# The first stage of a fused two-block transformer kernel, reordered: where the condition row, the squares, the weight splits and the first transfers are done

## The reference, cut to what matters

```python
c_act = silu(c)                                    # c: one row of 1024
mod = (c_act @ w_ada + b_ada).reshape(1, 3, 3, 1024)   # shift, scale, gate of 3 sublayers
u = rmsnorm(h, norm1_g) * (1 + mod[:, 0, 1]) + mod[:, 0, 0]
g, up = split(u @ w_gu_1, 2)                       # 1024 -> 2 x 2816
h = h + 0.5 * mod[:, 0, 2] * ((silu(g) * up) @ w_down_1)
u = modulate(rmsnorm(h, norm2_g), mod[:, 1, 0], mod[:, 1, 1])
proj = u @ w_mix_in                                # queries, keys, values, convolution, gates
```

## Time and profile before

| | |
|---|---|
| time, median of 3 runs | 2076.58 us |
| profiled execution: its time / span | 2077.91 us / 2075.9 us |
| TensorE busy | 2039.7 us (98%) |
| VectorE / ScalarE / GpSimd busy | 53% / 39% / 6% |
| chain that ended last | TensorE 91%, VectorE 3%, issue 2%, DMA 1% |
| mean granted clock | 0.993 |

### The profile page before, as it was taken

The page is one execution under the profiler, slowest core; times in us unless marked ns, Lnnn a source line. Parts: engine busy times, 40 slices in busy tenths (PEclk is TensorE's granted clock), DMA queues, the critical chain, the costliest instruction groups (busy, mean ns, idle before and its releaser), DMA issues.

```text
span 2075.9 us, 25090 instructions
## 1 busy us (share of the span) xinstructions
PE 2039.7 (98%) x10215; PEld 1706.4 (82%) x10215; DVE 1101.8 (53%) x1681; ACT 804.4 (39%) x1252; POOL 116.0 (6%) x139
## 2 busy tenths in 40 slices
PE   6999999999999999999999999999999999999997
PEld 4788888888878898888889887778888988888887
DVE  8744444577753553333335646665425475456546
ACT  4422232355554343222323436555323353234334
POOL 3100000200000010000002000000000100000012
PEclk8999999999999999999999999999999999999999
DMA  7744534443433223233222332222333232332241
GB/s 278 254 165 158 177 137 134 152 142 121 142 94 101 92 75 108 76 112 106 89 70 90 119 122 72 73 81 92 102 99 94 72 102 83 111 102 95 71 149 41
DMA packets 71202, 236.27 MB, mean 114 GB/s; under 512 B 8864, under 2 KB 11168, under 8 KB 70704
## 3 DMA queue, kind: packets, MB, share of 16 engines
q1 hardware_dynamic: 68912, 226.59, 32.6%
q0 software_dynamic: 2032, 7.90, 1.3%
q10 hardware_dynamic: 144, 0.18, 0.0%
HBM read 229.89 MB, written 4.75 MB: 113 GB/s over the span
## 4 chain that ended last, share of the span: by engine, by line
PE 91%; DVE 3%; issue 2%; DMA 1%; ACT 1%; POOL 1%; DVEq 0%; SPq 0%; POOLq 0%; ACTq 0%
PE bank L678 81%; PE bank L742 4%; PE bank L1086 1%; PE bank L1072 1%; PE bank L968 1%; PE bank L859 1%; PE bank L862 1%; DVE raw_m L1635 1%; POOL ssq L2257 0%; DMA w_raw<-in_w_gu_dram 0%; PE bank L998 0%; DMA w_raw<-in_w_mix_dram 0%; PE bank L773 0%; DVE w_raw L1635 0%; PE bank L1118 0%
## 5 line engine op out<-in xcount | busy, mean ns | idle before, releaser
L1639 DVE TENSOR_TENSOR w_lo<-w_raw,w_hi 128x1024 fp32r<-128x1024 f32 (+2 forms) x367 | 418.2, 1167 | 202.1 <-ACT w_hi L1183 201.5
L678 PE MATMUL bank<-u_hi,w_hi 128*128 128x512 f32 (+1 forms) x1920 | 497.6, 372 | 7.1 <-ACT ple_s L1361 3.5
L678 PE MATMUL bank<-u_lo,w_hi 128*128 128x512 f32 (+1 forms) x1920 | 495.5, 371 | 7.0 <-DVE u_lo L1939 4.9
L678 PE MATMUL bank<-u_hi,w_lo 128*128 128x512 f32 (+1 forms) x1920 | 495.8, 370 | 0.0
L1183 ACT ACTIVATE w_hi<-w_raw 128x1024 fp32r<-128x1024 f32 (+2 forms) x368 | 347.2, 976 | 257.6 <-PE bank L678 193.4
L678 PEld LDWEIGHTS bank<-u_hi,w_hi 128*128 128x128 f32 x1920 | 358.0, 190 | 68.9 <-ACT ple_s L1361 3.9
L678 PEld LDWEIGHTS bank<-u_lo,w_hi 128*128 128x128 f32 x1920 | 357.5, 189 | 68.6 <-DVE u_lo L1939 5.7
L678 PEld LDWEIGHTS bank<-u_hi,w_lo 128*128 128x128 f32 x1920 | 357.3, 189 | 58.4
L1767 DVE TENSOR_TENSOR ff_a<-ff_s,bank 128x512 f32<-128x512 f32 x44 | 30.2, 687 | 224.0 <-issue 211.7
L1259 ACT ACTIVATE act_hi<-ff_a 128x512 fp32r<-128x512 f32 x66 | 41.7, 632 | 257.9 <-DVE ff_a L1767 217.8
L678 PE MATMUL bank<-act_lo,w_hi 128*128 128x512 f32 (+1 forms) x561 | 131.1, 379 | 0.0
(11 more groups left out here) (275 smaller groups left out, 2083.5 us busy)
## 6 DMA issues: line engine op xcount, KB each, us to landing
w_raw<-in_w_gu_dram SPq DMA_DIRECT2D x127, 512.0 KB, 3.9
w_raw<-in_w_ada_dram SPq DMA_DIRECT2D x66, 512.0 KB, 4.5
w_raw<-in_w_dn_dram SPq DMA_DIRECT2D x48, 384.0 KB, 3.1
w_raw<-in_w_mix_dram SPq DMA_DIRECT2D x36, 512.0 KB, 3.6
w_raw<-in_w_dn_dram SPq DMA_DIRECT2D x48, 320.0 KB, 3.2
w_raw<-in_w_in_dram SPq DMA_DIRECT2D x24, 512.0 KB, 3.7
w_raw<-in_w_o_dram SPq DMA_DIRECT2D x16, 512.0 KB, 3.5
w_raw<-in_w_in_g_dram SPq DMA_DIRECT2D x16, 512.0 KB, 3.6
```

What stands on the lines that cost most here:

```text
L678: m = e.matmul(bank[b][:, c], w, (x.lo if part == 2 else x.hi)[:, k, c], start=start, stop=stop, skip_group_check=True)
L1639: e.tensor_tensor(lo_of(name), raw_of(i), f32(hi_of(name)), ALU.subtract).then_inc(*s_w_lo.inc(name))
```

## The change

The condition row is loaded as one row by ScalarE's queue, put through silu there, and spread over the partitions by TensorE (two matmuls with a row of ones) and two VectorE copies. ScalarE squares all chunks into buffers of their own, VectorE adds them in four pairs, TensorE sums the pairs over partitions (16 small matmuls). VectorE's `first_normed` multiplies by the inverse norm alone; ScalarE computes the gain, applies scale and shift in one pass, and rounds; VectorE subtracts for all d. GpSimd does none of these any more. The first ring has 13 buffers and is used twice; the gate and up part of the first sublayer then uses a ring of eight, all later ones the ring of four. The embed weights and 1g3, 1u3 get split buffers of their own. TensorE gets matmuls on the identity (`warm`) at four places, and the order of the first groups is written out. In the stream 1g3 and 1u3 come ahead of the three "a" items; four "a" items now stand behind mv0 to mv3.

The diff, cut:

```diff
-N_MORE = 14
+N_MORE = 9
+FIRST_STREAM = (("pt", "ple0", "a", "a", "ple1", "1g0", "1u0", "a", "a", "1g1", "1u1", "a", "a", "1g2", "1u2")
+                + 10 * ("a",) + ("1g3", "1u3"))
+FIRST_STEPS = ((0, 0), ("embed", 7), ("warm", 8), (0, 1), (1, 0), (1, 1), ("warm", 6), (2, 0), (2, 1),
+               *[(g, k) for k in range(2, 8) for g in range(3)])
...
                     weight(f"{tag}u{m}", io[w_gu][NFF + m])
-                between()
+                    between()
...
-    ffn_tiles("1", "w_gu_1", "w_dn_1", first=3, between=some_ada)
+    ffn_tiles("1", "w_gu_1", "w_dn_1", first=4, between=some_ada)
     for j in (12, 16, 13, 17):
         weight(f"m{j}", io["w_mix"][j])
     for k in range(4):
         weight(f"mv{k}", io["w_mix_v"][k])
+        some_ada()
```

TensorE (`open_bank(b)` waits for whoever frees the bank; a bank written by `embed(d)` is free once ScalarE's `embed(d)` has copied it out):

```diff
+        def warm(n, b):
+            open_bank(b)
+            q.wait_ge(s_ident, 0)
+            for _ in range(n):
+                e.matmul(bank[b][:, 0:P], ident[:, :], ident[:, :], start=True, stop=True, skip_group_check=True)
+
         def embed(d):
-            b = banks.next()
+            b = banks.next() if d < 7 else 7
...
-            frees[b] = [(s_embed_dve if d < 2 else s_embed_act, d)]
+            frees[b] = [(s_embed, d)]
...
+        warm(16, 5)
+        q.wait_ge(s_crow, 0)
+        for x in range(2):
+            m = e.matmul(bank[6 + x][:, :], one_row[:, :], c_row[:, T * x:T * (x + 1)], start=True, stop=True,
                          skip_group_check=True)
...
+        warm(12, 5)
+        embed(0)
+        embed(1)
+        for k in range(0, ND, 2):
+            q.wait_ge(s_ssq_dve, ("n0", k))
+            for i in range(NB):
+                m = e.matmul(bank[7][:, i:i + 1], first_sq[:, k, P * i:P * (i + 1)], ones[:, :], start=k == 0 and i == 0,
...
+        embed(2)
...
+        for d in (3, 4, 5, 6):
             embed(d)
...
+        for g, i in FIRST_STEPS:
+            if g == "warm":
+                warm(i, 7)
+            elif g == "embed":
+                embed(i)
+            else:
+                if g == len(groups):
+                    groups.append(first_group(g))
+                groups[g](i)
```

ScalarE:

```diff
+        def first_high(d):
...
+            e.activation(gmul[:, d:d + 1], mod[:, g:g + 1], ACT.Identity, scale=vec("norm1_g", d),
...
+            q.wait_ge(s_u0, ("n0", d))
+            q.wait_ge(s_ada, c)
+            e.activation(x, x, ACT.Identity, scale=gmul[:, d:d + 1], bias=mod[:, c:c + 1]).then_inc(*s_u_hi.inc(("n0+", d)))
+            q.wait_ge(s_u_hi, ("n0+", d))
+            e.activation(u_hi[:, d, :], x, ACT.Copy).then_inc(*s_u_hi.inc(("n0", d)))
+
+        split_hi()
+        embed(0)
+        split_hi()
+        first_high(0)
+        embed(1)
         embed(2)
         embed(3)
         split_hi()
         split_hi()
+        first_high(1)
+        embed(4)
+        embed(5)
+        split_hi()
+        split_hi()
+        embed(6)
+        first_high(2)
+        first_high(3)
+        embed(7)
+        first_high(4)
+        first_high(5)
+        split_hi()
+        first_high(6)
+        split_hi()
+        first_high(7)
```

VectorE:

```diff
+        prepare_up_to("ple0")
+        for x in range(2):
+            q.wait_ge(s_out, ("c", None))
+            e.tensor_copy(cact[:, T * x:T * (x + 1)], bank[6 + x][:, :]).then_inc(*s_cact.inc(x))
+        for d in range(0, ND, 2):
...
+            e.tensor_tensor(a, a, b, ALU.add).then_inc(*s_ssq_dve.inc(("n0", d)))
...
+        prepare_up_to(mod_col(0, 1, 0))
         q.wait_ge(s_rt, ("n0", 0))
         e.reciprocal(inv[:, :], rt[:, :]).then_inc(*s_inv.inc(("n0", 0)))
+        prepare_up_to("ple1")
+        first_normed(0)
+        prepare_up_to(mod_col(0, 0, 1))
+        first_low(0)
+        prepare_up_to(mod_col(0, 1, 1))
+        first_normed(1)
+        prepare_up_to("1u1")
+        first_low(1)
+        prepare_up_to(mod_col(0, 1, 2))
+        first_normed(2)
+        prepare_up_to(mod_col(0, 0, 3))
+        first_low(2)
+        prepare_up_to(mod_col(0, 1, 3))
+        for d in range(3, ND):
+            first_normed(d)
+            prepare_up_to(mod_col(0, 1, d + 1) if d < ND - 1 else "1u3")
+            first_low(d)
```

More of the change, by code:

```diff
@@ L25 @@
 N_RAW = 4
-N_MORE = 14
+N_MORE = 9
 N_SPLIT = 6
-N_DVE = 3
+N_EARLY = 3
 VEC = {}
@@ L518, in block_kernel, with raw_place @@
     size = {x[1]: x[3] for x in stream}
-    by_pool = ("1g0", "1u0", "1g1", "1u1", "1g2", "1u2")
-    def raw_of(i):
-        n = stream[i][3]
-        return raw_more[i][:, 0:n] if i < N_MORE else w_raw[(i - N_MORE) % N_RAW][:, 0:n]
+    raws = raw_more + w_raw + raw_ffn
+    wide = (9, 10, 11, 12, 8, 13, 14, 15)
+    first_end = 2 * (N_MORE + N_RAW)
+    wide_end = first_end + (stream_index["1u21"] + 1 - first_end) // len(wide) * len(wide)
+    def raw_place(i):
+        if i < first_end:
+            return i % (N_MORE + N_RAW)
+        if i < wide_end:
+            return wide[(i - first_end) % len(wide)]
+        return N_MORE + (i - wide_end) % N_RAW
+    def raw_of(i):
+        return raws[raw_place(i)][:, 0:stream[i][3]]
+    raw_before, split_place, split_before = {}, {}, {}
+    last_at = {}
+    for i in range(len(stream)):
+        raw_before[i] = last_at.get(raw_place(i))
+        last_at[raw_place(i)] = i
+    last_at = {}
+    ring = [name for name in names if name not in EARLY]
+    for name in names:
+        split_place[name] = N_SPLIT + EARLY[name] if name in EARLY else ring.index(name) % N_SPLIT
+        split_before[name] = last_at.get(split_place[name])
+        last_at[split_place[name]] = name
+    hi_tiles, lo_tiles = w_hi + x_hi, w_lo + x_lo
     def hi_of(name):
-        return w_hi[split_index[name] % N_SPLIT][:, 0:size[name]]
+        return hi_tiles[split_place[name]][:, 0:size[name]]
     def lo_of(name):
-        return w_lo[split_index[name] % N_SPLIT][:, 0:size[name]]
+        return lo_tiles[split_place[name]][:, 0:size[name]]
     def split_end(name):
-        return min(split_index[name] + 1 + N_SPLIT, len(names))
+        j = split_index[name] + 1
+        while j < len(names) and (split_before[names[j]] is None or split_index[split_before[names[j]]] <= split_index[name]):
+            j += 1
+        return j
     def stream_end(name):
@@ L909, in first_group @@
             return outer(["1" + x for x in FIRST_OUTS[2 * g:2 * g + 2]], first_u, banks, glu_freed("1"))
[L911 to L917 removed]
+        groups = []
+        for g, i in FIRST_STEPS:
[3 more added lines that the diff above has]
+                embed(i)
+            else:
+                if g == len(groups):
+                    groups.append(first_group(g))
+                groups[g](i)
         def constant(x):
@@ L1897, in vector_program @@
         e.memset(eps[:, :], EPS).then_inc(*s_const.inc("eps"))
+        e.memset(one_row[:, :], 1.0).then_inc(*s_const.inc("row"))
         for i, x in enumerate((1.0, EPS, 1.0)):
             e.memset(sum_w[:, i:i + 1], x).then_inc(*s_const.inc(("sum_w", i)))
-        prepare()
-        prepare()
-        for d in range(ND):
-            add_square("n0", d)
-            if d in (4, 6):
-                i = d // 2 - 2
-                q.wait_ge(s_out, (("emb", i), None))
-                e.tensor_copy(ple_s[0][:, i, :], psum(("emb", i))[:, :]).then_inc(*s_embed_dve.inc(i))
@@ L1908, in vector_program, with first_normed, first_low @@
-        prepare()
-        q.wait_ge(s_cact, 0)
+        def first_normed(d):
+            q.wait_ge(s_out, ("inv", "n0", 0))
+            if d >= 4:
+                q.wait_ge(s_u_lo, ("n0", d - 4))
+            e.tensor_tensor(u0_full[d % 4][:, :], hres[:, d, :], bank[6][:, :], ALU.mult).then_inc(*s_u0.inc(("n0", d)))
+        def first_low(d):
+            q.wait_ge(s_u_hi, ("n0", d))
+            e.tensor_tensor(u_lo[:, d, :], u0_full[d % 4][:, :], f32(u_hi[:, d, :]),
+                            ALU.subtract).then_inc(*s_u_lo.inc(("n0", d)))
@@ new lines, in prepare_up_to @@
+        def prepare_up_to(name):
+            while done["stream"] <= stream_index[name]:
+                prepare()
+        prepare_up_to("ple0")
[3 more added lines that the diff above has]
+        for d in range(0, ND, 2):
+            a, b = first_sq[:, d, :], first_sq[:, d + 1, :]
+            q.wait_ge(s_sq, ("n0", d + 1))
+            e.tensor_tensor(a, a, b, ALU.add).then_inc(*s_ssq_dve.inc(("n0", d)))
@@ L2413, in sync_program @@
             e.dma_start(hres[:, 2 * i:2 * i + 2, :], io["xt"][:, 2 * i:2 * i + 2, :]).then_inc(*s_x[i].inc(0, by=16))
-        e.dma_start(cact[:, :], io["c"].to_broadcast([P, D])).then_inc(*s_c.inc(0, by=16))
-        load_beyond("1u3")
+        while done["load"] <= stream_index["1u6"]:
+            load()
         for i in range(2):
-            q.wait_ge(s_ple_out, i)
+            q.wait_ge(s_ple_out[i], 0)
         e.dma_start(ws_s[:, :, :], io["ws"]).then_inc(*s_ws_in.inc(0, by=16))
```

186 lines of the change are left out of this document (67 added, 119 removed).

## The result

| | before | after |
|---|---|---|
| median, lowest and highest of 5 runs, us | 2076.58 (2074.25 to 2079.43) | 2082.47 (2081.79 to 2087.47) |
| ratio after/before, 95% interval | | 1.0033 [1.0017, 1.0049] |
| span of the profiled execution, us | 2075.9 | 2080.7 |
| mean granted TensorE clock | 0.993 | 0.993 |

The change made the kernel slower: by 5.9 us or 0.28% between the medians, by 0.33% in the ratio, which weighs all the runs. Forecast were 2082.0 and 0.26%, by the median.

The account below looks back on a forecast made before the run. TensorE, busy 98% of the span, was taken as the bound. Opening -2.0 us and moved "a" items +7.3 gave +5.3: 2083.2 profiled, so 2082.0 by the median, range 2074.5 to 2087.5.

Parts of the forecast that it names:

- the likeliest case: Whole kernel: main line, slower by 0.26% at 2082.0 us, own range 2079 to 2086; chance 0.53.
- Until the inverse norm: Opening on TensorE up to the inverse's spreading: ends at 20.2 us instead of 20.6, bringing 0.4 us.
- Rival C: Opening: identity calls do not raise the clock, schedule and mark shift 3 to 6 us, time 2085 to 2088; chance 0.13.
- VectorE's list: Eight chunks of the opening: first_normed(3) ends at 39.1 us, last low part about 57, products about 1.28 us.
- The bank-7 wait: Opening: TensorE's warm(8) waits for ScalarE's copy of embed 7, idling 12.9 us from 28.3 to 41.2.
- the mark: End of 1u7 on TensorE, closing the opening: 132.5 us instead of 134.5, 2.0 us won.
- rival B: Opening: bank's wait does not hold TensorE, 1u7 ends at 117.4, 17.1 us won, time 2066.8; chance 0.07.
- (a): Boundary, second half's chunks 2 to 3: two more VectorE products delay chunk 3's low part, 1.4 us lost.
- (b): Values' stage before the scores: two more transfers of 1.7 us delay the values' copies, 3.4 us lost.
- (c): Scores: TensorE's wait grows from 0.95 to 4.35 us and slow matmuls follow, 2.5 us lost.
- Rival A: Values' stage absorbs the moved products, leaving 1.4 and at most 1 us lost against 2.0 won: 2077; chance 0.25.

Follow-up runs that it names:

- e10: Kernel after without the two late groups of identity calls and with the four "a" items in the first sublayer's pairs 4 to 7: 2064.38 us, ratio 0.9937.
- e9: Kernel after without the two late groups of identity calls (8 and 6 calls into bank 7): 2070.96 us, ratio 0.997.
- e11: e10 also without the two early groups of identity calls (16 and 12 calls): 2060.87 us, ratio 0.9923.
- e4: Kernel before with only four "a" items moved from pairs 7 to 10 of the first sublayer to behind mv0 to mv3: 2085.30 us, ratio 1.0032.
- e5: Kernel after with "a" items kept behind mv0 and mv1 only, the other two in pairs 4 and 5: 2080.38 us, ratio 1.0009.
- e6: Kernel after with "a" items kept behind mv2 and mv3 only, the other two in pairs 4 and 5: 2082.74 us, ratio 1.003.
- e12: e10 with embed 1 put between the one-column sums, splitting them into two pieces: 2063.53 us, ratio 0.9931.
- e1: Kernel after with ScalarE's copy of embed 7 moved ahead of first_high(2) and first_high(3): 2077.30 us, ratio 0.9999.
- e2: Kernel after with the four "a" items moved back into the first sublayer's pairs 4 to 7: 2077.94 us, ratio 1.0001.
- e3: Kernel after with both the copy of embed 7 moved earlier and the four "a" items in the first sublayer: 2070.68 us, ratio 0.9957.

## Why the prediction was right, and which terms were off

The forecast of 2082.0 was met at 2082.47, and the likeliest case was the one that came: slower, by two groups of causes that the experiments take away one by one. In part the closeness is luck, for terms that were off cancel. The sum was +5.3 us; the spans of the two profiled executions differ by 4.8, the medians by 5.9. Term by term:

- **Until the inverse norm** the text had 20.2 us and a gain of 0.4; it ended at 21.5. Up to the end of the sums the forecast held (18.0, measured 17.95) by two errors that cancel: the full speed came not at 8 but at about 5.2 (from there an identity instruction takes 0.11 us instead of 0.21), within the first group, which ended at 7.0; and the row (1.9 us), the 12 calls (2.7) and the 16 sums (3.5) each took longer than put. The missing 1.3 us are embed 2 and the inverse: behind the sums the clock fell to half, from 18.9 to 22.3 us, which no term had. With the later course the inverse ends at 24.0 to 24.4. There the step "so I let the full speed begin at 8" holds for the row (7.7 to 9.6 in e10) and fails for the second group and its 3.4 us at half speed. Rival C, that the calls do not raise the clock, is refuted as it stands, but its price, a mark 3 to 6 us later, is about what the later course costs (3.2 to 4.9).
- **VectorE's list**: `first_normed(3)` was to end at 39.1 and ended at 40.2, after a start 1.5 us later than put (21.9, not 20.4); the last low part ended at 57.6 against about 57. Products took 1.27 to 1.30 us. Right.
- **The bank-7 wait** was to last 12.9 us, from 28.3 to 41.2; it lasted 12.03, to 42.3. Its start moved by the 1.3 us of the inverse and the slow matmuls behind it, its end by VectorE's later start. Then 378 matmuls (85.7 us), 14 calls (2.8) and the slow clock give the mark at 133.3, so 133.3 - 42.3 - 85.7 - 2.8 = 2.5 are left for the slow clock, where 2.8 was taken. (The granted clock is 0.50 until 46.2, which accounts for 1.9 of them.) The mark was put at 132.5: 2.0 us won were 1.2. e9 shows the cause directly, and the time that rival B gave for its absence: it had the mark at 117.4 and 17.1 us of gain over the kernel before, e9 has 120.4 with the later opening, and e11, which has neither calls nor that opening, 117.4.
- **(a)** 1.4 us were 1.15 to 1.2 by the wait (after, e4, e5). Measured from S1, the scores' first part begins 1.4 us later (456.77 - 405.2 against 456.57 - 406.4), so the term was right as a whole.
- **(b)** 3.4 us: TensorE's wait grew from 0.95 to 5.08, 4.1 us. The size is near, the mechanism was not the one written. The prediction took 8.5 / 5 = 1.7 us for each transfer from three landings and multiplied it by two more. But the chain shows what the issues wait for: each load needs a buffer that VectorE frees, and behind the pause VectorE now runs a product and a low part more, 2.35 us, before the load at 446.5; that load takes 4.53 us instead of 3.51, 1.0 more. Together they put the issue of m18 3.6 us later (454.6, not 451.05), and its transfer took 5.67 us instead of 4.91. That 2 x 1.7 comes out near 3.6 is luck; the upper bound of 4.4, "where VectorE's products lie between", named what happens.
- **(c)** 2.5 us were 1.6: from the scores' start to the first matmul on `negtri` it took 475.17 - 462.53 = 12.6 us, before 469.23 - 458.20 = 11.0. The wait was longer than supposed, but the half speed after it was over at about 466, after 3.5 us and not 5. The model was misread: the 5.05 slow us behind the idle time of 4.27 in the earlier trace rows are the end of a longer slow stretch of the kernel before, which had begun ahead of that idle time (TensorE alone, columns as above):

```profile
28.00:40.00 12.00, 7.30 (x16) 0.50 0.41 163
```

1.4 + 4.1 + 1.6 is the 7.1 measured. So (b) was put too small by 0.7, (c) too large by 0.9, and the sum came out at 7.3. The Trainium skill's figures for the DMA rate ("DMA: Bandwidth & Descriptors", opening table), by which (b) would have been 2.4 or 2.9, are not tested by this, for 2.35 of the 3.6 us are VectorE's work. (In 446 to 452 us the kernel after moved 345 GB/s.)

Rival A (the stage absorbs the items) is refuted by e4, e5 and e6. In the prediction's account of (b) one step was only half said: "the freed buffers first take m8 and an 'a' item that were in before" is right, but it hangs on the two items behind mv2 and mv3 alone, as e5 and e6 show; the two others are free but for (a).

## What to carry to other kernels

An engine that executes in order waits for whatever stands next in its list, useful or not: filler work to keep a clock up needs a destination that is already free, or it becomes the wait that lets the clock fall; leaving out 14 such calls was worth 11.5 us here. When work is moved along a stream with few buffers, ask what will lie in the buffers while the consumer is busy elsewhere: two items placed on one side of such a pause cost 1.2 us, and two on the other 6.1. And before calls are added to raise the clock, count what they delay: work at half speed that begins 5.9 us earlier was worth more than full speed later.

## What the runs showed of the hardware that was not expected

- 32 one-column matmuls in one piece (3.6 us) were followed by 3.4 us at granted clock 0.50, with no idle time before (18.9 to 22.3 us in the kernel after, 20.3 to 23.7 in e10). In two pieces of 1.84 us with six large matmuls between and behind they were not (e12). In the trace TensorE counts as busy all the time; its clock did not follow that.
- The same kernel's opening takes one of two courses, 24 identity instructions in 2.94 or in 4.57 us (two and seven of nine profiles), so that a comparison of two kernels by one profile each can be wrong by 3 us and more at the start.
- Idle times of 5.08 us (after), 3.90 (e1), 4.1 (e4) and 1.9 (e2) were each followed by matmuls at granted clock 0.50, for 3.5 to 5.6 us, as was one of 1.97 before. Idle times of 1.7 us (e3), 0.81 and 0.42 (e9) were not. But neither was one of 2.76 in e4, before the pair 1g4, where the granted clock is 1.00: the length of the idle time alone does not tell.
